# Pairing the transposes of keys and values, a new order on VectorE at the start of each block, and the last transposes of x in one run

## What is computed

```python
h = rmsnorm(x, g_norm)
u_p, z_p, q, k, v, z_r, gates = split(h @ w_in)            # 1024 x 10240
pooled = multi_scale_pool(u_p)                             # windows 2, 4, 8, 16
y_pool = (pooled * silu(z_p)) @ w_branch_pool
q, k = rope(q), rope(k) * 256 ** -0.5                      # 4 heads, 256 wide; v is 512 wide
# per head, in chunks; s is the state (256 x 512)
o = (q @ k.T * decay) @ v + (q * gamma**(i+1)) @ s
s = gamma**C * s + (k * gamma**(C-1-i)).T @ v
o = groupnorm(o) * gn_ret
y_ret = (o * silu(z_r)) @ w_branch_ret
x_out = x + (sigmoid(g_p) * y_pool + sigmoid(g_r) * y_ret) @ w_out
y = rmsnorm(x_out, g_final)
```

## Time and profile before

| | |
|---|---|
| median of 3 runs | 2850.07 us |
| the profiled execution | 2851.84 us |
| its span | 2850.0 us |
| TensorE matmul busy | 2803.0 us, 98% |
| VectorE busy | 1808.7 us, 63% |
| ScalarE busy | 1127.2 us, 40% |
| GpSimd busy | 685.1 us, 24% |
| mean granted TensorE clock | 0.996 |

### The profile page before, as it was taken

One profiled execution on the slowest core, in us unless ns is written; L12 is line 12 of the kernel. 1 busy time (PEld: TensorE's weight loads), 2 busy tenths in 40 slices (PEclk: granted clock), 3 DMA queues, 4 the chain that ended last, 5 costly groups with the idle time before them and its releaser, 6 DMA issues.

```text
span 2850.0 us, 36714 instructions
## 1 busy us (share of the span) xinstructions
PE 2803.0 (98%) x13504; PEld 2252.7 (79%) x13504; DVE 1808.7 (63%) x2588; ACT 1127.2 (40%) x1901; POOL 685.1 (24%) x456
## 2 busy tenths in 40 slices
PE   6999999999999999999999999999999999999998
PEld 5888888888877777777777787877887788778876
DVE  7657566667555365555666656775677667766775
ACT  5444444444564433443444433333333333333332
POOL 4343433435332233434343320000000000000000
PEclk9999999999999999999999999999999999999999
DMA  4544444444564344453544456477547754775496
GB/s 143 192 148 154 172 148 155 158 175 150 177 231 141 112 153 161 163 183 110 194 143 151 158 238 251 163 270 306 210 163 267 305 215 160 270 297 223 154 341 254
DMA packets 281849, 552.80 MB, mean 194 GB/s; under 512 B 24216, under 2 KB 166872, under 8 KB 270527
## 3 DMA queue, kind: packets, MB, share of 16 engines
q1 hardware_dynamic: 266279, 541.73, 53.3%
q10 hardware_dynamic: 15168, 8.46, 1.0%
q0 software_dynamic: 224, 0.26, 0.0%
HBM read 375.59 MB, written 175.14 MB: 193 GB/s over the span
## 4 chain that ended last, share of the span: by engine, by line
PE 92%; DVE 4%; issue 2%; DMA 1%; ACT 1%; POOL 1%; ACTq 0%; SPq 0%; DVEq 0%; POOLq 0%
PE bank L1309 29%; PE bank L1311 28%; PE bank L1310 28%; PE bank L1359 2%; PE bank L1382 1%; PE bank L1501 1%; DVE w_lo L2172 1%; PE bank L1631 1%; DVE xa_lo L2172 0%; PE bank L1619 0%; PE bank L1609 0%; DVE xs L2186 0%; PE bank L1304 0%; DMA x_d<-x_out 0%; DMA raw<-in_w_branch_pool 0%
## 5 line engine op out<-in xcount | busy, mean ns | idle before, releaser
L1309 PE MATMUL bank<-xa_hi,wa_hi 128*128 128x512 f32 x2240 | 889.7, 397 | 4.6 <-ACT part_s L1863 3.1
L1310 PE MATMUL bank<-xa_lo,wa_hi 128*128 128x512 f32 x2240 | 874.2, 390 | 0.0
L1311 PE MATMUL bank<-xa_hi,wa_lo 128*128 128x512 f32 x2240 | 874.2, 390 | 0.0
L1309 PEld LDWEIGHTS bank<-xa_hi,wa_hi 128*128 128x128 f32 x2240 | 421.2, 188 | 107.2 <-issue 22.7
L1311 PEld LDWEIGHTS bank<-xa_hi,wa_lo 128*128 128x128 f32 x2240 | 420.9, 188 | 90.4
L1310 PEld LDWEIGHTS bank<-xa_lo,wa_hi 128*128 128x128 f32 x2240 | 421.5, 188 | 82.9
L2172 DVE TENSOR_TENSOR wa_lo<-w_raw,wa_hi 128x512 fp32r<-128x512 f32 x320 | 312.7, 979 | 166.0 <-ACT wa_hi L1856 165.2
L2172 DVE TENSOR_TENSOR wa_lo<-w_sum,wa_hi 128x512 fp32r<-128x512 f32 x240 | 194.2, 809 | 241.3 <-ACT wa_hi L1856 241.3
L2172 DVE TENSOR_TENSOR w_lo<-raw,w_hi 128x512 fp32r<-128x512 f32 (+1 forms) x288 | 181.9, 658 | 197.1 <-ACT w_hi L1970 197.1
L1856 ACT ACTIVATE wa_hi<-w_raw 128x512 fp32r<-128x512 f32 x320 | 201.1, 628 | 242.5 <-PE bank L1311 238.3
L1970 ACT ACTIVATE w_hi<-raw 128x512 fp32r<-128x512 f32 (+1 forms) x288 | 166.6, 603 | 315.2 <-PE bank L1311 222.7
(11 more groups left out here) (253 smaller groups left out, 4322.9 us busy)
## 6 DMA issues: line engine op xcount, KB each, us to landing
w_raw<-in_w_in SPq DMA_DIRECT2D x80, 1024.0 KB, 5.3
v_d<-turned SPq DMA_DIRECT2D x64, 512.0 KB, 3.2
qk_s<-qk_d SPq DMA_DIRECT2D x32, 1024.0 KB, 7.5
v_s<-v_d SPq DMA_DIRECT2D x32, 1024.0 KB, 11.6
raw<-in_w_branch_ret SPq DMA_DIRECT2D x128, 256.0 KB, 4.7
tabs<-in_c_rope SPq DMA_DIRECT2D x16, 1024.0 KB, 6.8
qk_d<-high SPq DMA_DIRECT2D x32, 512.0 KB, 4.6
qk_d<-c_low SPq DMA_DIRECT2D x32, 512.0 KB, 5.4
```

The costliest lines, as they stand in the source:

```text
L1309: pe.matmul(out, lh, rh, start=first, stop=False, skip_group_check=onto)
L1310: pe.matmul(out, lh, rl, start=False, stop=False, skip_group_check=onto)
L1311: return pe.matmul(out, ll, rh, start=False, stop=last, skip_group_check=onto)
```

## The change

On TensorE in stage A, the turns stand in pairs behind products 2 and 4, and the transposes of operands 5 and 6 of x's last group both stand ahead of product (0, 1). On VectorE in stage B, the row of each block's first head puts `statistics` and `output_bias` of its second chunk between the pieces of the next head's scores, and `final` goes from the middle of the row to its end; on SyncE `results` goes from ahead of the loads of head 2 to behind them and two units. For hb = 1 the low parts of the first four units, which stood at the end of hb = 0, stand around `gate_og(0)`, behind `new_state(1, 0)` and ahead of `statistics(1, 0)`.

```diff
@@ SyncE
                     head_inputs(b, 1)
-                    results(b - 1)
                 for h in range(1, HEADS):
                     if h + 1 < HEADS:
                         head_inputs(b, h + 1)
                     ahead(b, (h - 1) * UH, (h - 1) * UH + 2)
+                    if b and h == 1:
+                        results(b - 1)
                     head_gates(b, h)
@@ TensorE
-                    if n == PAIRS - 1 and i >= PROD - 3:
-                        one_product(0, i - (PROD - 3))
+                    if n == PAIRS - 1 and i == PROD - 3:
+                        one_product(0, 0)
             for j in range(ALL):
                 for i in range(PROD):
-                    if j or i >= 3:
+                    if j or i:
                         one_product(j, i)
-                    if j and kind(j - 1) in ("k", "v") and 1 <= i < 5:
+                    if j and kind(j - 1) in ("k", "v") and i in (2, 4):
+                        turn(j - 1, i - 2)
                         turn(j - 1, i - 1)
@@ VectorE
                     new_state(hb, 0)
+                    if hb == 1:
+                        for u in range(2):
+                            low(u)
+                        gate_og(hb - 1)
+                        for u in range(2, RAW):
+                            low(u)
                     statistics(hb, 0)
-                    if h:
+                    if hb > 1 and h:
                         gate_og(hb - 1)
...
                     new_state(hb, 1)
-                    if b and h == 0:
-                        final(b - 1)
...
-                    if h + 1 < HEADS:
+                    if h == 0:
+                        mask_scores(hb + 1, 0)
+                        scores_low(hb + 1, 0)
+                        mask_scores(hb + 1, 1)
+                        statistics(hb, 1)
+                        scores_low(hb + 1, 1)
+                        output_bias(hb, 1)
+                        if b:
+                            state_low(hb + 1, 0)
+                            final(b - 1)
+                    elif h + 1 < HEADS:
                         mask_scores(hb + 1, 0)
                         mask_scores(hb + 1, 1)
                         scores_low(hb + 1, 0)
                         scores_low(hb + 1, 1)
                         if b:
                             state_low(hb + 1, 0)
-                    statistics(hb, 1)
                     if h:
+                        statistics(hb, 1)
                         lows(b, (h - 1) * UH + 4, 1)
-                    output_bias(hb, 1)
-                    if hb == 0:
-                        for u in range(RAW):
-                            low(u)
+                        output_bias(hb, 1)
```

## The result

The changed kernel takes 2853.91 us (median of 20 runs, 2852.88 to 2856.03), the one before 2850.11 in the same series (20 runs). The ratio is 1.0015, with an interval of [1.0008, 1.0021]: 3.8 us slower (2.3 to 6.0), where the forecast was 0.1 faster. The profiled execution is 2853.72 us with a span of 2851.9. That is near its median, while the profiled execution of before lies 1.7 above its own: in it TensorE's clock is at the lower level for 10.24 us around the first products, in the one after for 3.41. So the two traces differ by 1.9 where the medians differ by 3.8, and a difference of up to 2 us between them in the first 55 us says nothing of the change.

A forecast was written before the change was run, and what follows sets the result against it. TensorE, busy 98% of the span, was taken as the bound; -3.9 (pairs, keys) - 1.3 (x) - 1.4 (block 0) + 6.5 (blocks 1 to 3) = -0.1 gave 2850.0 us, own range 2847 to 2853, stated 2844.0 to 2856.5.

The forecast's parts named there:

- TensorE's part: Stage A, TensorE's two edits: -3.9 us for turns in pairs and keys, -1.3 for x's last transposes.
- block 0's row: VectorE's reordered row in block 0: earlier statistics shorten TensorE's waits, -1.4 us (0 to -4.9).
- blocks 1 to 3, stores with them: Later `st_lo` and gate make TensorE wait, 2.2 us a block, +6.5 in all; stores on SyncE cost 0.
- the gain is -1.4: Block 0: TensorE will stand 2 to 3 us for y at `branch(0, 1)`, so only 1.4 us are gained.
- rival C: Clock falls behind new waits in blocks 0 to 3 make it slower, 2856.6 us for all; chance 0.10.
- statistics to bias 2.51 (the second low part lies inside GpSimd's time): VectorE, blocks 1 to 3: this stretch keeps its 2.51 us, so `state_low` starts at 1991.6 against 1990.68.
- Cost 0: SyncE, blocks 1 to 3: late stores delay y but TensorE doesn't wait; at the late end 1 us a block.
- barely covered: Blocks 1 to 3: y comes by 2023, TensorE needs it at `branch(4, 1)` at 2022.5.
- Rival D: Stores hold SyncE longer, units 7 and 8 and y come late: +2 us a block, 2856; chance 0.06.
- pairs and keys: Stage A: 48 pairs of turns give 2.9 us (1.7 to 4.8), 8 jobs of keys 1.0 (0 to 1.0).
- Rival E: Pairs give nothing, the switch being inside the transposes' own time: +3.9 us, 2854; chance 0.07.
- x's 1.3: Start: earlier transposes of x remove the wait for `part_s` at product (0, 2), -1.3 us (0 to -1.4).

The follow-up runs named there:

- block0_only: Kernel before plus TensorE's two edits and the new VectorE row of block 0, blocks 1 to 3 and SyncE as before: 2846.59 us, ratio 0.9985.
- y_first: block0_only with y's copies for hb = 1 ahead of the low parts that wait for weights: 2841.13 us, ratio to before 0.9965.
- stores_late: Kernel before plus TensorE's two edits and the stores at the changed late place on SyncE, VectorE's rows as before: 2857.21 us, ratio 1.0021.
- changed_y_first: The whole change with y's copies at each block's second head ahead of the low parts that wait for weights: 2847.85 us, ratio to before 0.9991.
- stores_late_y: stores_late with y's copies at each block's second head ahead of the low parts that wait for weights: 2843.39 us, ratio to before 0.9975.
- final_stores_early: The whole change with `final` and the stores both back where they stood before: 2856.68 us, ratio to before 1.0019.
- pairs_alone: Kernel before with only the turns in pairs on TensorE, all else as before: 2847.45 us, ratio to before 0.9986.
- final_late: Kernel before plus TensorE's two edits, `final` behind `state_low` but ahead of the statistics, and stores late: 2862.15 us, ratio 1.0040.
- final_early: The whole change with `final` back behind `new_state(hb, 1)`, stores still late: 2856.6 us, ratio to before 1.0021.
- block0_before: The whole change with block 0's VectorE rows (hb = 0 and 1) as before: 2854.04 us, ratio to before 1.0014.
- changed_st_first: The whole change with `state_low` ahead of the statistics on VectorE and `state_high` likewise on ScalarE: 2859.24 us, ratio to before 1.0029.

## Why the prediction was wrong

The forecast was -0.1, the result +3.8. The -0.1 is a gain of 6.6 less a loss of 6.5, so what was missed in the terms, 0.4, 2.0 and 1.6, all the same way, makes the whole result. By its terms, each against what the experiments gave:

| term | forecast | measured |
|---|---|---|
| TensorE's part | -5.2 | -4.8 |
| block 0's row | -1.4 | +0.6 |
| blocks 1 to 3, stores with them | +6.5 | +8.1 |

**The step that failed most is "the gain is -1.4" for block 0.** Its path was right up to `branch(0, 1)`: the train of weights moved only with its start, the copies of y came 6.88 us earlier in the trace (1737.23 to 1730.35), of which 5.4 is stage A, and a new wait of 3.5 us stood where I put 2 to 3. What the term left out is behind it: a wait of that size brought the lower clock, which cost 1.7 us here and 2.2 in block0_only, where nothing hides it. The fall that before had at 1720 to 1725 was ahead of `branch(0, 1)`, where y was late anyway (copies until 1739.71, TensorE at 1739.89), so it cost next to nothing. Now it comes behind that point. In the trace the start of `branch(0, 1)` gained 1.6 beyond stage A's shift, and the fall took 1.7. y_first, where y's copies come first and both the wait and the fall are gone, is 5.8 below block0_only, each against its before: wait and clock are what block 0 lost. That the term is +0.6 and not nearer 0 rests on a difference within the noise and on one pair of traces. I had put the clock into rival C as a chance, for the new wait in block 0 too, when it belonged into the term.

**Blocks 1 to 3: the mechanism held, the size was 1.6 short (0.8 by the two traces).** Forecast were a wait for `st_lo` of 1.9 and one for `z_in` of 1.3; they are 2.2 and 1.26. The step "statistics to bias 2.51 (the second low part lies inside GpSimd's time)" was 0.4 short: it took 1983.33 to 1986.22, 2.89, because the low part (0.69) and a wait of 0.59 for GpSimd stand there in a row, where before there was one wait of 0.81. Three times 2.2 - 0.98 + 1.26 is 7.4; a clock fall in block 2 swallowed one wait for `z_in` and cost a little more than it.

**"Cost 0" for the stores held only in company.** The step says that y comes at 2023 at the latest and is needed at 2022.5, "barely covered". The 2022.5 had the 2.2 us in it that TensorE loses at `st_lo` and `z_in`. Without that loss the same stores cost 11 (stores_late), three waits of 1.8 to 2.4 and a clock fall of 1.7 at each. The row costs 7.3 where y isn't late (changed_y_first against y_first; the stores are late there, but stores_late_y shows that they cost nothing without the wait for y). Together they cost 8.1 and not 18: VectorE's row makes TensorE 2.5 late in each block, SyncE's stores make y 1.8 to 2.4 late, and one hides the other. The new row with the stores alone put back was not run. Shrinking `final` gained little in part for that reason. Putting `final` back gained nothing for another: with the statistics early the row is as slow with the stores early as with them late (final_stores_early). Rival D had the right mechanism, and its price came out neither alone (3.7 a block) nor in company (none seen).

**The pairs and x.** The forecast was 3.9 for pairs and keys; pairs_alone measured 4.1, with 2.6 to each side. The jobs came out at 22.1 for both kinds, as written, so a pair gives 0.05 (0.10 in a job of two), and I had 0.06. Rival E is out. x's 1.3 is 1.57 by two traces with the same clock; by the times it is 0.7, within the noise. (The list of TensorE's waits adds up to 38.5 us, not to some 37; nothing rests on it.)

**Where the rule on queues stands.** The Trainium skill, "DMA: Bandwidth & Descriptors", section "Queues, rings and completion order", was cited for stores that can't overtake the head's inputs. It says that descriptors of a ring are taken in order; it does not say that they finish in order. The runs agree with it, 2.8 us to land ahead of these inputs, 15.9 behind them, but don't prove it: DMA engines that are full, in whatever order, would delay the stores too. The other rule that the prediction cited, "TensorE: Matmul & The Clock Gate", section "Part 4: PE-mode transpose" of the Trainium skill, that transposes don't count for the clock, was not tested by itself. The falls in blocks 1 to 3 that it would explain came, in final_late at the transposes of `og`, but they came as well behind `st_lo` in final_early, where products follow.

## What to carry over

When an engine's order is written by hand, look first for pieces that are ready but stand behind a piece that waits for a DMA: one such move (y's copies) was worth 5 to 14 us here, more than the whole change. Two delays of the same size on different engines hide each other, so "costs nothing" has to be worked out with every other term of the sum taken away, and an experiment that undoes one of them alone can show nothing. A wait of some 2 us on TensorE may bring a clock fall, and each of 3 us and more did here, so the price of the fall belongs into the term, unless something later is late anyway.

## What the runs showed of the hardware

- In blocks 0 to 3 the granted clock fell to 1.2 GHz in or within 1.2 us behind all 15 waits of TensorE of 3.09 us and more in these traces, and at none of the single ones of 0.98. At seven waits for y of 1.8 to 2.4 us it fell six times. Behind the `st_lo` waits of 2.2 us it fell in 6 of 15, with the same work around them; in the change in block 2 and not in block 1. In block 0 the waits of 1.56 and 2.31 in a row were followed by a fall in every trace that has them. A fall costs 1.7 us, or up to 3.1 where it lasts twice as long (block0_before: clock 0.69 over the 10 us behind a wait); the part that lies in the wait costs nothing, which left 2.2 in block0_only above. What decides at some 2 us is open.
- The first 55 us differ by up to 2.2 us between traces of kernels with the same code there: product (0, 3) starts at 49.65 to 49.98 where the lower clock has ended before the first product (at 40.6), and at 51.28 to 51.83 where it reaches into it. A difference of that size at the start says nothing.
- A store of 512 KB landed in 2.8 us ahead of the loads of head 2, and in a median of 12.6 (changed_st_first) to 16.1 us (final_early) in the kernels that issue it behind them.
